# The queries' operand of a differential attention layer, made together with that of keys and values

## The chip, the cores and the metric

The kernel runs on one core of one Trainium2 chip. The core has a matrix engine (PE, whose weight loads are listed apart as PEld), a vector engine (DVE), a scalar engine (ACT), a general engine (POOL) and an engine that issues the weight DMAs (SP); each follows its own list of instructions in order, and they meet through semaphores. The metric is the device time of one execution in microseconds (us). Lower is better.

## The reference, cut to what matters

A block of four attention branches is followed by a convolution layer and a differential attention layer, each with memory attention and a gated feed-forward layer behind it. The sequence has 256 tokens, the model 1024 features. The change touches the differential layer:

```python
def shared_kv(x, kv_norm, w_k, w_v, cos, sin):
    h = rms_norm_2(x, kv_norm)
    k = apply_partial_rope((h @ w_k).reshape(B, S, 8, 2, 64), cos, sin)
    v = (h @ w_v).reshape(B, S, 8, 128)
def diff_attention(h, k, v, ...):          # h = rms_norm_2(x, norm_mix[1]), the same x
    q = apply_partial_rope((h @ w_q).reshape(B, S, 8, 2, 64), cos, sin)
    # per head: two softmaxes over 64 features, p0 - lam * p1, times v; a norm; @ w_o
```

Keys, values and queries are made of the same `x`, with the same root of the mean square, and of two gains, `kv_norm` and `norm_mix[1]`.

## The kernel before, in words

**Products.** Every operand of a product is split into a high and a low part, and a product is three products of parts. Weights come through four raw slots in the order of `weight_plan`, in chunks of 512 rows by 512 columns. For each chunk SP issues the load, ACT copies the high part (`act_chunk`, L591), DVE makes the low part (`vec_chunk`, L601), two chunks ahead of PE, and PE multiplies (L669). ACT may only split a chunk when PE has left the chunk three places ahead of it. A step below is one chunk on PE.

**A norm in front of a product.** `x` is not scaled first. `Norm.pe_turn` turns `x` on PE, 128 by 128 at a time into the `small` banks (L816), four transposes a call; ACT writes the high part of `x` times the gain (L834), DVE the low part (L846). The roots are multiplied in behind the product. `H` is one place for all such operands one after another; an operand's half may be written when the one before it has been taken by PE.

**The differential layer, before.** PE multiplies keys (`w_k`, four steps), values (`w_v`, four), queries of heads 0 to 3 (`w_q` 0, two steps) and of heads 4 to 7 (`w_q` 1, two). Keys and values read the operand `kv`. Behind the values `x` is turned again, for the operand `q` with the other gain: half 0 inside the values' last step, half 1 inside the queries' first. ACT copies products out scaled by the root (L2882 for keys and queries, L3016 for values). Keys and queries are then rotated by DVE in `attended` (L2894 to L2900), turned by PE (L731) and copied to `k_t` or `q_t` by ACT (L2875). ACT's copies of the second queries out of their product, the next split and the copies to `q_t` stand in one turn of its list.

**Groups.** Attention runs in six groups of heads (`DIFF_GROUPS`): for each half of the heads, heads 0, 1 with the later 128 tokens, heads 2, 3 with the same, then four heads with the first 128. A group has stages: PE makes scores (L2957); DVE adds the mask, takes maxima and their negatives (L3151 to L3155) for both softmaxes; ACT takes exponentials (L3072); DVE's part two makes reciprocals and the difference (L3160 to L3166); PE turns the rows (L2965); ACT copies them (L1479); PE mixes the values (L2973); ACT copies out (L3081). `weave` runs the groups in rounds: in each round each engine's list has one stage of every group under way, the start of a new group, and one step of filling. On PE and DVE the filling is the last thing in a round, on ACT the first. Counting from 0, group g starts in round g; its rows are turned in round g + 2 and its values mixed in round g + 3. The filling before is the last step of `w_q` 1, then eight steps of keys and values of the memory attention, then the steps of the output projection. When three groups are done, `finish_half` norms that half of the heads (DVE, POOL L766 to L771, DVE L3188), turns it (PE L731) and writes the projection's operand; for the second half its transposes on PE stand in round 10.

**Banks.** Four `small` banks go round in the order in which PE takes them; PE waits until the use four places earlier is released.

Of the kernel before, what the change touches and what calls it, by code (L numbers as in the profile page):

```python
# [124 lines left out]
def weight_plan(w):  # L125
# [64 lines left out]
    memory_use(0)  # L190
    feed(0)
    square(w["w_k_shared_2"])
    square(w["w_v_shared_2"])
    even(w["diff_w_q_2"][0])
    memory(1)
    square(w["diff_w_o_2"][0])
    memory_use(1)
# [91 lines left out]
class Kernel:  # L289
# [84 lines left out]
    def layout(self):  # L374
        w = self.w
        self.limit = self.top - 4 * FIRST_W
        self.vector_cols = self.sb("vector_cols", [P, N_VECTOR_ROWS])
        self.to_line()
        self.whole_conv = self.sb("whole_conv", [P, KT, S], at=self.at + 4 * KT * S)
        parts = self.sb("H", [P, 2, KT, S], F32R)  # L380
        h = parts[:, 0, :, :], parts[:, 1, :, :], parts[:, :, :, :]
        names = ["first", "merged", "conv", "ln", "mem0", "ffn0", "kv", "q", "att", "mem1", "ffn1"]
        ops = {name: Operand(name, h, before) for before, name in zip([None, *names], names)}
        self.H_first, self.H_merged, self.H_conv, self.H_ln, self.H_kv, self.H_q, self.H_att = (
            ops[name] for name in ("first", "merged", "conv", "ln", "kv", "q", "att"))
        self.H_mem, self.H_ffn = ([ops[f"{name}{layer}"] for layer in range(2)] for name in ("mem", "ffn"))
        self.w_raw = [self.sb(f"w_raw{i}", [P, CK * CN]) for i in range(self.N_RAW)]
        self.w_high, self.w_low, self.w_first, self.rooms, self.used, self.st = [], [], [], [], [], {}
        for slots, name, more in ((self.w_high, "w_high", HIGH_ROOM), (self.w_low, "w_low", LOW_ROOM)):
            for i in range(self.N_SPLIT):  # L390
                self.room(LINE // 4 - more)
                if slots is self.w_high:
                    self.w_first.append(self.sb(f"w_first{i}", [P, CK * CN], at=self.at))
                slots.append(self.sb(f"{name}{i}", [P, CK * CN + more], F32R))
        self.X, self.HN = self.sb("X", [P, NT, D]), self.sb("HN", [P, NT, D])
        self.gains_at = self.at
        self.gains = [self.sb(f"gain{i}", [P, D]) for i in range(2)]
        self.common = self.sb("common", [P, COMMON_W])
        self.ident, self.ones, self.causal, self.invfreq, self.half = (
            self.common[:, at:at + n] for at, n in (COMMON[name] for name in ("ident", "ones", "causal", "invfreq", "half")))  # L400
        self.room(432)
        self.vector_rows = self.sb("vector_rows", [N_VECTOR_ROWS, P])
        at, self.vcol = 0, {}
        for name, (*_, n) in VECTORS.items():
            self.vcol[name] = self.vector_cols[:, at:at + n]
            at += n
        self.two_roots, self.neg_lam, self.c_silu = self.stat("two roots", 2 * NT), self.stat("neg lambda", 1), self.stat("c silu", KT)
        for name in ("cos", "sin", "cos angle", "sin angle"):
            self.stat(name, NT * ROT // 2)

        def bank(name):
            return self.ctx.enter_context(self.nc.psum_tensor(name, [P, 512], F32))
        self.product = Ring("product", [bank(f"product{i}") for i in range(4)])
        self.small = Ring("small", [bank(f"small{i}") for i in range(4)])
        common_end = self.at
        self.layout_condition()
        self.at = self.after_gate
        self.layout_branches()
        self.limit = (self.top - 8 * KT * S) // LINE * LINE
        self.mem_op = Operand("mem", self.pair("mem", KT, at=self.limit))  # L420
        self.at = common_end
        self.layout_second()
        self.norms = {
            ("mem", 0): Norm(self, "mem0", self.H_mem[0]), ("ffn", 0): Norm(self, "ffn0", self.H_ffn[0]), ("after", 0): Norm(self, "kv", self.H_kv),
            ("q", 1): Norm(self, "q", self.H_q, "kv"), ("mem", 1): Norm(self, "mem1", self.H_mem[1]), ("ffn", 1): Norm(self, "ffn1", self.H_ffn[1]),
            ("after", 1): Norm(self, "final"),
        }

# [345 lines left out]
class Norm:  # L774
# [65 lines left out]
    def vec_turn(self, n):  # L840
        V = self.k.vec
        for b in range(2):
            key = (self.name, n, b)
            V.wait_ge(self.x.free(n), ("turned", key), ("operand high", key))
            for hi, lo, ps, gain in self.turned(n, b):
                V.eng.scalar_tensor_tensor(lo, ps, gain, hi.bitcast(F32), ALU.mult, ALU.subtract).then_inc(  # L846
                    *V.tells("operand_low", self.x.ready(n), self.k.small.free(key)))


WIDE_PLACES, NARROW_PLACES = (9, 13), (16, 24)  # L850
# [1423 lines left out]
def act_feed(k, layer, beside=None):  # L2274
# [41 lines left out]
    for n in range(D // CN):  # L2316
        for step in range(-(-FT // CK)):
            act_chunk(k)
            if n == 1 and step == 0 and after.x:
                after.act_turn(0)  # L2320
        if n == 0 and after.x:
            after.act_squares(n)
        if not after.x:
# [7 lines left out]
def vec_feed(k, layer, beside=None):  # L2331
# [92 lines left out]
    for n in range(D // CN):  # L2424
        for step in range(-(-FT // CK)):
            vec_chunk(k)
            if n == 1 and step == 0 and after.x:
                after.vec_turn(0)
        for t in range(NT):
            if after.x:  # L2430
                vec_add(k, (("down", layer, n), t), ("products", ("down", layer, n)), after, n, t, norm.root(t), ("root", norm.name))
# [481 lines left out]
def pe_differential(k):  # L2913
    pe = k.pe
    for step in pe_square(k, "w_k", k.H_kv, k.norms["after", 0].pe_behind(0, 1, WIDE_PLACES)):
        if step == 3:
            for t in range(NT):
                pe_turn_heads(k, "k heads", 0, t)
    for step in pe_square(k, "w_v", k.H_kv, k.norms["q", 1].pe_behind(3, 0, (4, 8))):
        if step == 0:  # L2920
            for t in range(NT):
                pe_turn_heads(k, "k heads", 1, t)

    def turn_queries(n):
        for t in range(NT):
            pe_turn_heads(k, "q heads", n, t)

    def queries(n):
        yield from pe_columns(k, ("w_q", n), k.H_q, KT, {(0, 15): lambda: turn_queries(0)} if n else k.norms["q", 1].pe_behind(0, 1, (4, 8)))

    told = {"groups": 0, "halves": 0}

    def fill():
        yield from queries(1)
        yield from pe_memory_keys(k, 1, ({(0, 26): lambda: turn_queries(1)}, {}))
        project = pe_add_to_x(k, "diff out", k.H_att, k.norms["mem", 1])
        for half in range(2):
            while told["halves"] <= half:
# [4 lines left out]
            yield  # L2943
        drain(project)
    filling = fill()
    drain(queries(0))
    next(filling)
    pe.wait_ge(("k heads", 1), "diff values")

    def group(heads, t):  # L2950
        nh, nk, key = len(heads), P * (t + 1), ("diff", heads[0], t)
# [14 lines left out]
        tr.then_inc(*pe.tells("turned", ("turned", key), k.rows.free((key, 0))))  # L2966
        yield
        bank, p = k.small.take((key, "mixed")), k.turned.of(key)
        pe.wait_ge(("turned rows", key), k.small.before((key, "mixed")))
        for i, h in enumerate(heads):  # L2970
            for j in range(t + 1):
                b = i * (t + 1) + j
# [18 lines left out]
def act_differential(k):  # L2991
    A = k.act
    for step in range(4):
        act_chunk(k)
        if step == 0:
            k.norms["after", 0].act_turn(1)
            k.norms["after", 0].act_squares(1)
        if step == 3:
            for t in range(NT):
                act_turn_heads(k, "k heads", k.k_t, 0, t)  # L3000
        if step >= 2:
            for t in range(NT):
                act_to_heads(k, "k heads", step - 2, t, ("w_k", 2 * (step - 2) + t), ("products", "w_k", step))
    for step in range(4):
        act_chunk(k)
        if step == 0:
            for t in range(NT):
                act_turn_heads(k, "k heads", k.k_t, 1, t)
        if step == 3:
            k.norms["q", 1].act_turn(0)  # L3010
        if step >= 2:
            n = step - 2
            for t in range(NT):
                bank = ("w_v", 2 * n + t)
                A.wait_ge(("root", "kv"), ("products", "w_v", step))
                A.eng.activation(k.vals[:, t, n * CN:(n + 1) * CN], k.product.of(bank)[:, 0:CN], ACT.Copy, scale=k.norms["after", 0].root(t)).then_inc(  # L3016
                    *A.tells("diff_values", "diff values", k.product.free(bank)))

    def turn_queries(n):
        for t in range(NT):  # L3020
# [2 lines left out]
    def rows_out(n):  # L3023
        for t in range(NT):
            act_to_heads(k, "q heads", n, t, (("w_q", n), t), ("products", ("w_q", n)), ("k heads", "turned"))

    told = {"groups": 0, "halves": 0}

    def fill():
        act_chunk(k)  # L3030
        turn_queries(0)
        yield
        act_chunk(k)
        yield
        rows_out(1)
        act_chunk(k)
        turn_queries(1)
        yield
        act_chunk(k)
        yield  # L3040
        act_keys_out(k, 1, 0)
        for out, n in ((act_keys_out, 1), (act_values_out, 0), (act_values_out, 1)):
            act_chunk(k)
            yield
            act_chunk(k)
# [9 lines left out]
            yield  # L3055
        drain(project)
    act_chunk(k)
    k.norms["q", 1].act_turn(1)
    act_chunk(k)
    rows_out(0)  # L3060
    filling = fill()
    next(filling)
    scale = HD ** -0.5

    def group(heads, t):
# [32 lines left out]
def vec_differential(k):  # L3098
    V = k.vec
    for step in range(4):  # L3100
        vec_chunk(k)
        if step == 0:
            k.norms["after", 0].vec_turn(1)
        if step >= 2:
            for t in range(NT):
                vec_rotate(k, "k heads", step - 2, t)
    for step in range(4):
        if step == 3:
            k.norms["q", 1].vec_turn(0)
        vec_chunk(k)  # L3110
    k.norms["q", 1].vec_turn(1)

    def queries(n):
        for step in range(2):
# [10 lines left out]

    def fill():
        yield from queries(1)
        yield from vec_chunks(k, 8)
        project = vec_add_to_x(k, "diff out", k.norms["mem", 1])
        for half in range(2):  # L3130
            while told["halves"] <= half:
# [5 lines left out]
        drain(project)  # L3137
    filling = fill()
    drain(queries(0))
    next(filling)  # L3140
    scale = HD ** -0.5

    def group(heads, t):
# [201 lines left out]
```

## Time and profile before

| what | value |
|---|---|
| device time, median of 3 runs | 1110.7 us (1110.38 to 1110.97) |
| span of the profiled execution | 1111.3 us, 0.6 above the median |
| PE busy | 98% of the span |
| DVE, ACT, POOL busy | 67%, 53%, 5% |
| mean DMA rate | 176 GB/s |
| granted clock of PE, mean | 0.997 of 2.4 GHz |

Busy time of PE counts pipelined products by their modelled ends, so short waits are best looked for in the list of waits and in the chain. The differential layer's products begin 698.5 us from the span's start and its projection ends near 862 us.

### The profile page before, as it was taken

Reading aid. Unit: us, or ns where it says so; the run is one execution under the profiler, and the core shown is the slowest. Engines: PE = TensorE matmul, PEld = TensorE weight load, DVE = VectorE, ACT = ScalarE, POOL = GpSimd, SP = SyncE. Lnnn points to the kernel's source line nnn. Section 1 sums busy time; section 2 is a strip of 40 time slices with the busy share of each in tenths; the row PEclk is TensorE's granted clock in tenths of the full one; section 3 lists DMA queues with packets and bytes.
Section 4 is the critical chain, followed back from the end, with each engine's and each line's share of the span. In section 5 each row is a group of like instructions: output and inputs, shape, how many; then the busy total and the mean of one; then the engine's idle time right before and its main releaser. Section 6 shows DMA issues by size and latency. Waiting matters only on the chain.

```text
span 1111.3 us, 15418 instructions
## 1 busy us (share of the span) xinstructions
PE 1092.0 (98%) x6251; PEld 951.6 (86%) x6251; DVE 749.5 (67%) x1024; ACT 583.6 (53%) x940; POOL 54.4 (5%) x87
## 2 busy tenths in 40 slices
PE   8999999999999999999999999999999999999997
PEld 6799988788898988989988988788988989888986
DVE  5736776865679977555678855546967546788643
ACT  3458653444477775555444544456765545444442
POOL 3311000000010000001000000000011000000000
PEclk9999999999999999999999999999999999999999
DMA  9956464655654325535555555544445435555550
GB/s 343 381 161 207 135 196 162 233 184 189 223 168 126 115 77 189 175 99 149 197 184 184 196 182 196 189 153 151 152 153 189 132 115 190 190 190 189 162 179 38
DMA packets 118776, 195.09 MB, mean 176 GB/s; under 512 B 6586, under 2 KB 39762, under 8 KB 118705
## 3 DMA queue, kind: packets, MB, share of 16 engines
q1 hardware_dynamic: 116144, 187.51, 50.7%
q0 software_dynamic: 2560, 6.60, 2.0%
q8 instruction: 49, 0.80, 0.3%
q14 instruction: 23, 0.18, 0.0%
HBM read 193.04 MB, written 1.05 MB: 175 GB/s over the span
## 4 chain that ended last, share of the span: by engine, by line
PE 83%; DVE 10%; ACT 5%; issue 1%; DMA 1%; POOL 1%; SPq 0%; DVEq 0%; ACTq 0%; POOLq 0%
PE product L669 55%; PE small L706 5%; PE product L706 5%; DVE conv_out L2719 5%; PE product L708 3%; PE small L708 3%; PE product L996 3%; ACT w_high L591 1%; ACT diagonal L2612 1%; DVE w_low L601 1%; PE small L816 1%; PE small L2081 1%; PE small L731 1%; PE small L1462 1%; PE small L1451 1%
## 5 line engine op out<-in xcount | busy, mean ns | idle before, releaser
L601 DVE TENSOR_TENSOR w_low<-w_raw,w_high 128x2048 fp32r<-128x2048 f32 (+3 forms) x160 | 350.0, 2190 | 180.2 <-ACT w_high L591 178.6
L591 ACT ACTIVATE w_high<-w_raw 128x2048 fp32r<-128x2048 f32 (+3 forms) x160 | 292.1, 1832 | 175.9 <-PE product L669 144.2
L669 PE MATMUL product<-w_high,H 128*128 128x512 f32 (+2 forms) x736 | 239.7, 393 | 0.5 <-DVE w_low L601 0.5
L669 PEld LDWEIGHTS product<-w_high,H 128*128 128x128 f32 x736 | 137.9, 188 | 26.9 <-DVE w_low L601 0.9
L669 PE MATMUL product<-H,w_high 128*128 128x256 f32 x816 | 150.9, 283 | 0.1
L669 PE MATMUL product<-w_low,H 128*128 128x512 f32 (+2 forms) x368 | 142.3, 387 | 0.0
L669 PEld LDWEIGHTS product<-H,w_high 128*128 128x128 f32 x816 | 126.6, 188 | 1.1 <-DVE w_low L601 0.5
L669 PE MATMUL product<-H,w_low 128*128 128x256 f32 x408 | 114.2, 280 | 0.0
L706 PE MATMUL product<-H,w_high 128*128 128x512 f32 x256 | 89.1, 391 | 0.0
L706 PE MATMUL small<-H,w_high 128*128 128x512 f32 x256 | 89.1, 391 | 0.0
L669 PEld LDWEIGHTS product<-w_low,H 128*128 128x128 f32 x368 | 69.3, 188 | 11.9 <-issue 0.2
L669 PEld LDWEIGHTS product<-H,w_low 128*128 128x128 f32 x408 | 76.8, 188 | 0.6 <-issue 0.2
L708 PE MATMUL product<-H,w_low 128*128 128x256 f32 x256 | 71.4, 279 | 0.0
L708 PE MATMUL small<-H,w_low 128*128 128x256 f32 x256 | 71.4, 279 | 0.0
L669 PE MATMUL product<-w_high,hidden_low 128*128 128x512 f32 x176 | 68.6, 390 | 0.0
L669 PE MATMUL product<-w_low,hidden_high 128*128 128x512 f32 x176 | 68.5, 389 | 0.0
L669 PE MATMUL product<-w_high,hidden_high 128*128 128x512 f32 x176 | 68.5, 389 | 0.0
L2719 DVE SCALAR_TENSOR_TENSOR conv_out<-conv_in,taps,conv_out 128x256 f32<-128x256 f32 x150 | 63.2, 478 | 1.2
L706 PEld LDWEIGHTS small<-H,w_high 128*128 128x128 f32 x256 | 48.1, 188 | 10.6
L706 PEld LDWEIGHTS product<-H,w_high 128*128 128x128 f32 x256 | 48.1, 188 | 10.5
L2519 PE MATMUL product<-whole_conv,w_raw 128*128 128x256 f32 x256 | 56.0, 379 | 0.0
L2519 PEld LDWEIGHTS product<-whole_conv,w_raw 128*128 128x128 f32 x256 | 48.3, 190 | 6.4
(412 smaller groups left out, 1784.3 us busy)
## 6 DMA issues: line engine op xcount, KB each, us to landing
w_raw<-in_ffn_w_gate SPq DMA_DIRECT2D x20, 1024.0 KB, 5.0
w_raw<-in_ffn_w_up SPq DMA_DIRECT2D x20, 1024.0 KB, 5.0
w_raw<-in_ffn_w_down SPq DMA_DIRECT2D x20, 1024.0 KB, 5.0
w_raw<-in_w_merge SPq DMA_DIRECT2D x16, 1024.0 KB, 5.2
w_raw<-in_w_ada SPq DMA_DIRECT2D x32, 256.0 KB, 6.5
w_raw<-in_mem_w_k SPq DMA_DIRECT2D x8, 1024.0 KB, 5.0
w_raw<-in_mem_w_v SPq DMA_DIRECT2D x8, 1024.0 KB, 5.0
w_raw<-in_conv_w_pw SPq DMA_DIRECT2D x16, 512.0 KB, 4.7
```

Of the source, the lines that this page charges most:

```text
L591: k.act.eng.activation(parts_of(k, i, j)[0], raw_of(k, i), ACT.Copy).then_inc(*k.act.tells("weights_high", ("weights high", i)))
L601: k.vec.eng.tensor_tensor(low, raw, high.bitcast(F32), ALU.subtract).then_inc(*k.vec.tells("weights_low", ("weights low", i)))
L669: mm = pe.eng.matmul(bank[:, off:off + wide], a, r, start=b not in started, stop=True, skip_group_check=True)
L706: pe.eng.matmul(bank[:, :].rearrange("p (i n) -> p i n", n=S), high[:, j, column], x.parts[:, :, first + j, :], start=first + j == 0, stop ...
L708: mm = pe.eng.matmul(bank[:, 0:S], low[:, j, column], x.high[:, first + j, :], start=False, stop=True, skip_group_check=True)
L731: tr = k.pe.eng.transpose(bank[:, i * P:(i + 1) * P], src[:, c:c + P], k.ident)
L816: tr = k.pe.eng.transpose(bank[:, j * S + t * P:j * S + (t + 1) * P], k.X[:, t, c:c + P], k.ident)
L996: mm = pe.eng.matmul(bank[:, off:off + wide], a, r, start=(name, b) not in begun, stop=True, skip_group_check=True)
L1451: mm = pe.eng.matmul(scores[:, i * nk:(i + 1) * nk], q[:, h, t * P:(t + 1) * P], kk_of(h)[:, 0:nk], start=i == 0, stop=True, skip_group_ch ...
L1462: mm = pe.eng.matmul(mixed[:, i * HD:(i + 1) * HD], p[:, b * P:(b + 1) * P], v_of(h, j), start=b == 0, stop=True, skip_group_check=True)
L2519: mm = pe.eng.matmul(bank[:, half * S:(half + 1) * S], raw[:, kt, half * P:(half + 1) * P], k.whole_conv[:, kt, :], start=kt + half == 0, ...
L2719: V.eng.scalar_tensor_tensor(y[:, f, :], src, wt, y[:, f, :], ALU.mult, ALU.add).then_inc(*V.tells("taps_vec", ("conv out", f)))
```

## The change

The operand `q` leaves the place `H` and gets one of its own, on the memory of `HN` and the two `gains` rows, which nothing else uses at that time. `x` is turned once. From the same `small` bank ACT and DVE make the operand `kv`, and then, one step later, the operand `q` with the other gain (`act_turn_queries`, `vec_turn_queries`: half 0 behind step 1 of the last feed-forward product, half 1 behind step 1 of the keys). The second norm object, with its sixteen transposes, is gone. Since queries no longer wait for values, the order of steps becomes: keys (four), queries 0, values 0, queries 1, values 1 (two each), and the weights load in that order. The queries' heads are turned inside the values' steps. The filling of the rounds becomes queries 1, values 1, then the memory's eight steps, then the projection. On ACT, the copies of the second queries to `q_t` move to the turn of filling behind the one with the copies out of the product.

```diff
-    square(w["w_v_shared_2"])
-    even(w["diff_w_q_2"][0])
+    for c in range(0, D, CN):
+        add(w["diff_w_q_2"][0], [(c, CN)])
+        add(w["w_v_shared_2"], [(c, CN)])
...
+        self.H_q = Operand("q", self.pair("H_q", KT, at=queries_at))
...
-            ("q", 1): Norm(self, "q", self.H_q, "kv"), ("mem", 1): Norm(self, "mem1", self.H_mem[1]), ("ffn", 1): Norm(self, "ffn1", self.H_ffn[1]),
...
+    def act_turn_queries(self, n):
+        A = self.k.act
+        for b in range(2):
+            A.wait_ge(("operand low", (self.name, n, b)))
+            for hi, _, ps, gain in self.queries(n, b):
+                A.eng.activation(hi, ps, ACT.Copy, scale=gain).then_inc(*A.tells("operand_high", ("queries high", n, b)))
+
+    def vec_turn_queries(self, n):
+        V = self.k.vec
+        for b in range(2):
+            V.wait_ge(("turned", (self.name, n, b)), ("queries high", n, b))
+            for hi, lo, ps, gain in self.queries(n, b):
+                V.eng.scalar_tensor_tensor(lo, ps, gain, hi.bitcast(F32), ALU.mult, ALU.subtract).then_inc(
+                    *V.tells("operand_low", self.k.H_q.ready(n), self.k.small.free((self.name, n, b))))
...
@@ pe_differential
-    for step in pe_square(k, "w_v", k.H_kv, k.norms["q", 1].pe_behind(3, 0, (4, 8))):
+    def values(n):
+        yield from pe_columns(k, ("w_v", n), k.H_kv, KT, {(0, 17): lambda: turn_queries(n)})
+    for step in queries(0):
         if step == 0:
             for t in range(NT):
                 pe_turn_heads(k, "k heads", 1, t)
+    drain(values(0))
     def fill():
         yield from queries(1)
-        yield from pe_memory_keys(k, 1, ({(0, 26): lambda: turn_queries(1)}, {}))
+        yield from values(1)
+        yield from pe_memory_keys(k, 1)
@@ act_differential
     def fill():
         act_chunk(k)
-        turn_queries(0)
         yield
         act_chunk(k)
         yield
         rows_out(1)
         act_chunk(k)
+        yield
         turn_queries(1)
-        yield
         act_chunk(k)
         yield
-        act_keys_out(k, 1, 0)
-        for out, n in ((act_keys_out, 1), (act_values_out, 0), (act_values_out, 1)):
+        values_out(1)
+        for out, n in ((act_keys_out, 0), (act_keys_out, 1), (act_values_out, 0), (act_values_out, 1)):
             act_chunk(k)
             yield
             act_chunk(k)
             yield
             out(k, 1, n)
...
+    turn_queries(0)
+    act_chunk(k)
+    values_out(0)
     filling = fill()
-    next(filling)
@@ vec_differential
     def fill():
         yield from queries(1)
-        yield from vec_chunks(k, 8)
+        yield from vec_chunks(k, 10)
...
     drain(queries(0))
-    next(filling)
+    drain(vec_chunks(k, 2))
```

In the changed list of PE, the mixing of a group also waits for the values of its half, and the scores of a group wait for the copies to `q_t` of its half, as before.

## Rows read from the trace of the kernel before

**Rows 1.** The page: busy time, share of the span and instructions of each engine.

```profile
PE 1092.0 (98%) x6251; PEld 951.6 (86%) x6251; DVE 749.5 (67%) x1024; ACT 583.6 (53%) x940; POOL 54.4 (5%) x87
```

**Rows 2.** Waits of PE, 745 to 820 and 820 to 900: total, times, longest.

```profile
PE small L2957 <- DVE drows L3151: 0.8, 1, 0.8
...
PE small L731 <- DVE attended L3188: 0.2, 1, 0.2
```

**Rows 3.** The chain that ended last, 741 to 763: start, us, what, count.

```profile
741.65 0.44 PE small L816 x4
742.09 0.94 PE product L669 x4
...
749.84 12.51 PE product L669 x55
```

**Rows 4.** Timeline of ACT, 679 to 752: start, us, what, [idle before, releaser].

```profile
679.72 1.92 ACT L591 ACTIVATE w_high<-w_raw 128x2048 fp32r<-128x2048 f32 x1 [2.59 <-PE product L669]
...
750.12 1.57 ACT L834 ACTIVATE H<-small,vector_cols 128x256 fp32r<-128x256 f32 x4
```

**Rows 5.** Timeline of DVE, 681 to 753.

```profile
681.66 2.29 DVE L601 TENSOR_TENSOR w_low<-w_raw,w_high 128x2048 fp32r<-128x2048 f32 x1 [2.08 <-ACT w_high L591]
...
751.09 1.66 DVE L846 SCALAR_TENSOR_TENSOR H<-small,vector_cols,H 128x256 fp32r<-128x256 f32 x4 [2.56 <-ACT H L834]
```

**Rows 6.** Timeline of DVE, 772 to 781.

```profile
772.84 0.23 DVE L2894 TENSOR_TENSOR rotated<-attended,stats 128x64 f32<-128x64 f32 x1 [3.12 <-ACT attended L2882]
...
774.85 2.28 DVE L601 TENSOR_TENSOR w_low<-w_raw,w_high 128x2048 fp32r<-128x2048 f32 x1
777.17 0.17 DVE L3160 RECIPROCAL stats<-stats 128x2 f32<-128x2 f32 x1
...
778.60 0.69 DVE L3151 TENSOR_TENSOR drows<-small,common 128x512 f32<-128x512 f32 x1
...
780.25 0.69 DVE L3151 TENSOR_TENSOR drows<-small,common 128x512 f32<-128x512 f32 x1
```

**Rows 7.** Timeline of ACT, 767 to 792.

```profile
767.31 1.28 ACT L3072 ACT_TABLE_LOAD   x1
...
772.05 1.27 ACT L2882 ACTIVATE attended<-product,stats 128x512 f32<-128x512 f32 x2 [1.21 <-PE product L669]
...
776.79 1.09 ACT L2875 ACTIVATE q_t<-small 128x512 f32<-128x512 f32 x2 [1.67 <-PE small L731]
...
787.19 0.40 ACT L3072 ACTIVATE drows<-drows,stats 128x128 f32<-128x128 f32 x1 [1.76 <-DVE stats L3155]
...
790.52 1.23 ACT L2030 ACTIVATE mem_keys<-product 128x512 f32<-128x512 f32 x2
```

**Rows 8.** The chain that ended last, 765 to 790.

```profile
765.28 1.07 PE small L2957 x8
766.35 5.68 PE product L669 x24
...
781.00 1.71 PE small L2957 x16
...
788.50 0.89 PE small L2973 x8
789.39 0.44 PE small L2965 x4
```

**Rows 9.** Timeline of ACT, 827 to 829.

```profile
827.34 1.91 ACT L591 ACTIVATE w_high<-w_raw 128x2048 fp32r<-128x2048 f32 x1 [2.84 <-PE product L669]
```

**Rows 10.** Timeline of DVE, 839 to 841.

```profile
839.80 0.69 DVE L3188 TENSOR_TENSOR attended<-attended,stats 128x512 f32<-128x512 f32 x1 [1.52 <-POOL stats L771]
```

**Rows 11.** Windows: us, busy us (instructions) PE, PEld, DVE, ACT, POOL, clock, DMA.

```profile
189.00:192.40 3.40, 3.40 (x14) 3.03 (x13) 2.46 (x12) 0.26 (x1) 0.00 (x0) 0.50 1.02 393
1100.00:1107.00 7.00, 4.73 (x21) 3.57 (x20) 2.25 (x3) 2.07 (x5) 1.44 (x3) 1.00 0.00 0
1107.00:1111.00 4.00, 0.00 (x0) 0.00 (x0) 0.75 (x1) 0.72 (x1) 0.72 (x2) 0.53 0.64 262
```

More of the change, by code:

```diff
@@ L381, in layout @@
         h = parts[:, 0, :, :], parts[:, 1, :, :], parts[:, :, :, :]
-        names = ["first", "merged", "conv", "ln", "mem0", "ffn0", "kv", "q", "att", "mem1", "ffn1"]
+        names = ["first", "merged", "conv", "ln", "mem0", "ffn0", "kv", "att", "mem1", "ffn1"]
         ops = {name: Operand(name, h, before) for before, name in zip([None, *names], names)}
-        self.H_first, self.H_merged, self.H_conv, self.H_ln, self.H_kv, self.H_q, self.H_att = (
-            ops[name] for name in ("first", "merged", "conv", "ln", "kv", "q", "att"))
+        self.H_first, self.H_merged, self.H_conv, self.H_ln, self.H_kv, self.H_att = (
+            ops[name] for name in ("first", "merged", "conv", "ln", "kv", "att"))
         self.H_mem, self.H_ffn = ([ops[f"{name}{layer}"] for layer in range(2)] for name in ("mem", "ffn"))
@@ L394, in layout @@
                 slots.append(self.sb(f"{name}{i}", [P, CK * CN + more], F32R))
-        self.X, self.HN = self.sb("X", [P, NT, D]), self.sb("HN", [P, NT, D])
+        self.X = self.sb("X", [P, NT, D])
+        queries_at = self.at
+        self.HN = self.sb("HN", [P, NT, D])
         self.gains_at = self.at
         self.gains = [self.sb(f"gain{i}", [P, D]) for i in range(2)]
+        self.H_q = Operand("q", self.pair("H_q", KT, at=queries_at))
+        assert queries_at % LINE == 0 and queries_at + 8 * KT * S == self.at
         self.common = self.sb("common", [P, COMMON_W])
@@ L424, in layout @@
             ("mem", 0): Norm(self, "mem0", self.H_mem[0]), ("ffn", 0): Norm(self, "ffn0", self.H_ffn[0]), ("after", 0): Norm(self, "kv", self.H_kv),
-            ("q", 1): Norm(self, "q", self.H_q, "kv"), ("mem", 1): Norm(self, "mem1", self.H_mem[1]), ("ffn", 1): Norm(self, "ffn1", self.H_ffn[1]),
+            ("mem", 1): Norm(self, "mem1", self.H_mem[1]), ("ffn", 1): Norm(self, "ffn1", self.H_ffn[1]),
             ("after", 1): Norm(self, "final"),
@@ L846, in vec_turn, with queries @@
                 V.eng.scalar_tensor_tensor(lo, ps, gain, hi.bitcast(F32), ALU.mult, ALU.subtract).then_inc(
-                    *V.tells("operand_low", self.x.ready(n), self.k.small.free(key)))
+                    *V.tells("operand_low", self.x.ready(n), ("operand low", key), self.k.small.free(key)))
+    def queries(self, n, b):
+        for j in range(2):
+            f = CK * n + 2 * b + j
+            q = self.k.H_q
+            yield q.high[:, f, :], q.low[:, f, :], self.k.small.of((self.name, n, b))[:, j * S:(j + 1) * S], self.k.vcol["q"][:, f:f + 1]
+    def act_turn_queries(self, n):
[11 more added lines that the diff above has]
+                    *V.tells("operand_low", self.k.H_q.ready(n), self.k.small.free((self.name, n, b))))
 WIDE_PLACES, NARROW_PLACES = (9, 13), (16, 24)
@@ L2320, in act_feed @@
                 after.act_turn(0)
+            if n == 1 and step == 1 and after.x:
+                after.act_turn_queries(0)
         if n == 0 and after.x:
@@ L2428, in vec_feed @@
                 after.vec_turn(0)
+            if n == 1 and step == 1 and after.x:
+                after.vec_turn_queries(0)
         for t in range(NT):
@@ L2918, in pe_differential @@
                 pe_turn_heads(k, "k heads", 0, t)
-    for step in pe_square(k, "w_v", k.H_kv, k.norms["q", 1].pe_behind(3, 0, (4, 8))):
-        if step == 0:
-            for t in range(NT):
-                pe_turn_heads(k, "k heads", 1, t)
     def turn_queries(n):
@@ L2928, in queries @@
     def queries(n):
-        yield from pe_columns(k, ("w_q", n), k.H_q, KT, {(0, 15): lambda: turn_queries(0)} if n else k.norms["q", 1].pe_behind(0, 1, (4, 8)))
+        yield from pe_columns(k, ("w_q", n), k.H_q, KT)
+    def values(n):
+        yield from pe_columns(k, ("w_v", n), k.H_kv, KT, {(0, 17): lambda: turn_queries(n)})
+    for step in queries(0):
+        if step == 0:
+            for t in range(NT):
+                pe_turn_heads(k, "k heads", 1, t)
+    drain(values(0))
     told = {"groups": 0, "halves": 0}
@@ L2945, in pe_differential @@
     filling = fill()
-    drain(queries(0))
-    next(filling)
-    pe.wait_ge(("k heads", 1), "diff values")
+    pe.wait_ge(("k heads", 1))
     def group(heads, t):
@@ L2968, in group @@
         bank, p = k.small.take((key, "mixed")), k.turned.of(key)
-        pe.wait_ge(("turned rows", key), k.small.before((key, "mixed")))
+        pe.wait_ge(("turned rows", key), ("diff values", heads[0] // 4), k.small.before((key, "mixed")))
         for i, h in enumerate(heads):
@@ L2997, in act_differential @@
             k.norms["after", 0].act_squares(1)
+        if step == 1:
+            k.norms["after", 0].act_turn_queries(1)
         if step == 3:
@@ L3003, in act_differential @@
                 act_to_heads(k, "k heads", step - 2, t, ("w_k", 2 * (step - 2) + t), ("products", "w_k", step))
[L3004 to L3017, printed above, removed]
     def turn_queries(n):
@@ L3025, in rows_out, with values_out @@
             act_to_heads(k, "q heads", n, t, (("w_q", n), t), ("products", ("w_q", n)), ("k heads", "turned"))
+    def values_out(n):
+        for t in range(NT):
+            bank = (("w_v", n), t)
+            A.wait_ge(("root", "kv"), ("products", ("w_v", n)))
+            A.eng.activation(k.vals[:, t, n * CN:(n + 1) * CN], k.product.of(bank)[:, 0:CN], ACT.Copy, scale=k.norms["after", 0].root(t)).then_inc(
+                *A.tells("diff_values", ("diff values", n), k.product.free(bank)))
     told = {"groups": 0, "halves": 0}
@@ L3057, in act_differential @@
     act_chunk(k)
-    k.norms["q", 1].act_turn(1)
+    for t in range(NT):
+        act_turn_heads(k, "k heads", k.k_t, 1, t)
     act_chunk(k)
     rows_out(0)
+    act_chunk(k)
+    turn_queries(0)
+    act_chunk(k)
+    values_out(0)
     filling = fill()
-    next(filling)
     scale = HD ** -0.5
@@ L3103, in vec_differential @@
             k.norms["after", 0].vec_turn(1)
+        if step == 1:
+            k.norms["after", 0].vec_turn_queries(1)
         if step >= 2:
@@ L3106, in vec_differential @@
                 vec_rotate(k, "k heads", step - 2, t)
[L3107 to L3111, printed above, removed]
     def queries(n):
@@ L3139, in vec_differential @@
     drain(queries(0))
-    next(filling)
+    drain(vec_chunks(k, 2))
     scale = HD ** -0.5
```

## Prediction

> **What bounds the kernel now.** I read the page first: PE is busy 98% of the span [rows 1], so time is won by giving PE less to do or by taking a wait of PE away, and lost by a new wait. Next the list of PE's waits over the differential layer: from 745 to 820 one entry stands there, the scores of group 2, held 0.8 us by DVE's mask; behind 820 one of 0.2 us, the last transposes of the attended rows, held by DVE's scaling [rows 2]. Then the chain through the layer, which is nearly all PE products, and last the timelines of ACT and DVE, to see in which order each comes to the work that PE waits for. The reader should see that ACT and DVE, though half idle, work down fixed lists: PE's two waits are waits for a place in DVE's list.
>
> **The transposes that go.** Four calls of four transposes leave PE: in the chain each is 0.44 us, and four products between two of them take 0.94 us, where 55 plain ones in 12.51 make 0.91 for four [rows 3]. That is 4 x 0.44 = 1.76, with the disturbance 4 x 0.03 more; bounds 1.76 and 1.88, I take 1.9. All of it lies on PE, where nothing covers it. A transpose costs 0.11 us here. The Trainium skill (TensorE: Matmul & The Clock Gate, Part 4: PE-mode transpose) gives about 0.275 us in a kernel for a bf16 one of the same size; by that figure sixteen would save 4.4 us and the sum below would come out near 1109.4 us. The rows decide here.
>
> **The work that moves.** ACT's and DVE's conversions for the queries stay as many: a half costs ACT 1.57 us [rows 4] and DVE 1.66 [rows 5]. For half 0 they move into the last feed-forward product, behind a split, where ACT was idle 2.59 us, until PE released a slot [rows 4], and DVE 2.08 us [rows 5]. DVE has 0.4 us to spare and its split is two chunks ahead of PE, so I put this at nothing; without that cover it would be at most 1.6. Half 1 goes into the keys, where the same cadence of steps leaves more. The loads change their order, not their number or size; SP's queue stays four slots ahead. At nothing, too: the new memory place, which has no earlier user to wait for.
>
> **The first rounds.** Let T be the end of PE's last product of queries 1. Before, that is 772.03 (766.35 + 5.68 [rows 8]) and lies in round 0; after, queries 1 fill rounds 0 and 1, so T ends round 1. The wait of 0.8 came because DVE, after T, had to rotate queries 1, split a chunk, do group 0's part two and only then reach group 1's mask [rows 6], whose bank group 2's scores take. After, part two of group 0 and the masks of group 1 stand in round 1 ahead of the rotation. This wait goes: -0.8. A range for it is 0 to 0.8.
>
> **The next wait.** What is late next is the copy to `q_t` of queries 1. DVE's list behind T is the same sequence with each group one higher: rotate at T + 0.8, split at T + 2.8, part two of group 1 at T + 5.1, masks of group 2 at T + 6.6 and T + 8.2 [rows 6]. ACT's list behind T is: copy the queries out (T + 0.0 to 1.3, 772.05 [rows 7]), split, turned rows of group 0, exponentials of group 2 (round 2), and only then, in round 3, the copies to `q_t`. The exponentials of a softmax start when its maxima are ready, one mask interval (1.65) behind its mask, and the eight of group 2 lasted 790.52 - 787.19 = 3.3 in two halves of 1.65 [rows 7]. So the last of them ends at T + 8.2 + 1.65 + 1.65 = T + 11.5, and the copies to `q_t` (1.09 [rows 7]) at T + 12.6. Before, the same copies ran at 776.79, which is T + 4.8, because they stood ahead of the exponentials.
>
> PE behind T: turn group 0's rows 0.44, scores of group 2 1.71 [rows 8], step 0 of values 1 with the queries' eight transposes (24 x 0.2275 = 5.46 [rows 3], and 0.88), mix group 0 0.89, turn group 1 0.44 [rows 8]: T + 9.8. Then it comes to group 3's scores, whose heads are those of queries 1, and stands until T + 12.6: **+2.8**. Queued behind it on PE are step 1 of values 1 and everything else. Lower bound 0.5, if DVE did its split of 2.28 ahead of the rotation; upper 4.5, if one more mask interval of 1.65 came in between; I take the list as it stands. In later rounds I see no further wait there: with each PE round over 6 us (5.68 + 0.89 + 0.44 [rows 8] and scores), ACT and DVE have caught up by round 4.
>
> Does ACT reach T in time? The first scores start 13.5 before T (two times 1.07 + 5.68 [rows 8]). From that start ACT copies values 0 out (about 1.2, like the queries' 1.27) and splits (1.9), then loads its table and does group 0's exponentials: 767.31 to 770.84 (772.05 less its 1.21 idle), 3.5 [rows 7], so 6.7. DVE's part two (1.43) and masks (3.3) of group 1 follow [rows 6], and a last half of exponentials about 1.2: 12.6. So ACT is free 0.8 to 0.9 ahead of T.
>
> **The end of the groups.** In round 8 ACT's turn of filling was a split alone, 827.34, right when PE ended a step [rows 9]; after, it begins with the memory keys' copies, 1.23 for two, the next operation 1.1 behind their start [rows 7]. Behind it queue the copies of group 5's output, from which a chain runs over DVE and POOL to the scaling at 839.80 [rows 10] that PE already waited 0.2 us for in round 10 [rows 2]. PE's cover (rounds 8 and 9) stays, so the shift comes on top: **+1.1**, with bounds 0 and 1.2. Before, the keys' and values' copies stood in the odd rounds; the two more steps of values have moved them to the even ones.
>
> **The sum.** -1.9 - 0.8 + 2.8 + 1.1 = +1.2 us. On the profiled span that is 1111.3 + 1.2 = 1112.5; that execution lies 0.6 above the median, so against the runs shown 1110.7 + 1.2 = **1111.9 us**. A difference up to 0.2% (2.2 us, about what a measurement of this kernel can tell from none) is called no change: 1108.5 to 1112.9.
>
> **The rivals.**
>
> *The saving survives.* If neither wait appears, PE gains 1.9 + 0.8 = 2.7: 1108.0 us, faster. For it: both new waits come from the order of ACT's list, and if ACT gets the copies to `q_t` done within PE's 9.8 us, nothing is lost. Against it: the exponentials of group 2 need maxima that DVE cannot give sooner than T + 8.2. If the first is away and only the second stays, it is 1109.1, still no change.
>
> *The clock falls in the new wait: slower.* PE's granted clock fell to half once in the kernel, for 3.4 us from 189.0, in a stretch of small products on a busy PE; and at the end, where PE's last product ended at 1104.73, it was full up to 1107 and at 0.53 (half for nearly all of it) in the four us behind [rows 11]. So 2.3 us of idle PE were borne, and somewhat more were not; the new wait of 2.8 lies there, and behind it come products. Price: 3.4 us at half (1.2 GHz) loses 1.7 us: 1113.6, which is where it passes 1112.9; a stretch of 2.0 us at half would be enough for that. Against it: in the layer itself the clock never fell, with a wait of 0.8. The Trainium skill (TensorE: Matmul & The Clock Gate, HAM oscillation) warns that idle gaps in front of matmuls bring the clock back to half; the end of this trace agrees, no row here shows it for a gap of this length between products.
>
> *ACT misses T.* If ACT's exponentials of group 1 run past T by x, the copies out, the rotation, and the copies to `q_t` all go x later, one for one. The margin is 0.8; from 1.0 more than that the sum passes 1112.9. For it: the chain to 12.6 is long; against it, every part of it is a row. Some 1114 at worst.
>
> **How the numbers follow.** Forecast (both waits, clock kept, 1110.6 to 1112.9): 0.55. Saving survives whole, around 1108.0: 0.13; in part, 1108.6 to 1110.5: 0.10. Clock falls, 1113.6: 0.14. ACT misses T, 1113 to 1114: 0.08. Faster 0.13, the same 0.55 + 0.10 = 0.65, slower 0.22. The range runs from the first rival's 1108.0 to the clock's 1113.8 (1113.6 and a little); it leaves out half of the first rival, and a part of the last two, under 0.2.
>
> **What would show it.** PE's transposes of `x` (L816) are sixteen fewer. Among PE's waits stands one of scores (L2957) on ACT's `q_t` (L2875), near 2.8 us, with ACT's copies some 12.6 us behind the end of queries 1; the scores' wait on DVE's mask is gone; the last transposes (L731) wait some 1.1 us longer on DVE's scaling. Wrong would be: no wait on `q_t`, a granted clock below full in the layer, or PE waiting for low parts of weights.

## The result

The changed kernel takes 1113.18 us (median of 17 runs, 1110.86 to 1115.98) where the kernel before takes 1110.76 (17 runs, 1110.02 to 1114.72). The ratio is 1.0018, 95% interval 1.0011 to 1.0025: 1.2 to 2.8 us more, 2.0 in the middle. (The ratio is not the quotient of the two medians, which is 1.0022.) The forecast was 1111.9, 0.1% more, in a range of 1108.0 to 1113.8. The median lies in that range, 1.3 us above the forecast and 0.3 us above 1112.9, where "no change" was to end. The ratio stays inside 0.2%; its interval excludes 1, so the changed kernel is slower.

### The profile page after: what moved, and what is told of

Same layout as the page of the kernel before. It is cut to its first block, busy times and chain, and to the rows that moved or that the text cites. A ratio compares the mean times of both kernels' runs of the same rounds, so it can differ in the third digit from the quotient of the medians.

```text
span 1114.7 us, 15383 instructions
## 1 busy us (share of the span) xinstructions
PE 1095.4 (98%) x6235; PEld 954.0 (86%) x6235; DVE 749.4 (67%) x1024; ACT 583.7 (52%) x940; POOL 54.1 (5%) x87
## 4 chain that ended last, share of the span: by engine, by line
PE 83%; DVE 9%; ACT 5%; issue 1%; POOL 1%; DMA 0%; SPq 0%; DVEq 0%; ACTq 0%; POOLq 0%
PE product L674 55%; PE small L711 5%; PE product L711 5%; DVE conv_out L2751 5%; PE product L713 3%; PE small L713 3%; PE product L1024 3%; ACT w_high L596 1%; ACT diagonal L2644 1%; DVE w_low L606 1%; PE small L2109 1%; PE product L977 1%; PE small L821 1%; PE small L736 1%; PE small L1490 1%
## 5 line engine op out<-in xcount | busy, mean ns | idle before, releaser
L674 PE MATMUL product<-w_high,H 128*128 128x512 f32 (+2 forms) x672 | 220.9, 396 | 0.5 <-DVE w_low L606 0.5
L674 PEld LDWEIGHTS product<-w_high,H 128*128 128x128 f32 x672 | 127.0, 190 | 24.9 <-DVE w_low L606 0.9
L674 PE MATMUL product<-w_low,H 128*128 128x512 f32 (+2 forms) x336 | 130.5, 388 | 0.0
L674 PEld LDWEIGHTS product<-w_low,H 128*128 128x128 f32 x336 | 63.8, 190 | 11.0 <-issue 0.2
```

The source lines that it names most:

```text
L674: mm = pe.eng.matmul(bank[:, off:off + wide], a, r, start=b not in started, stop=True, skip_group_check=True)
```

## The profile after

The page of the changed kernel: PE has sixteen instructions fewer than in [rows 1].

```profile
span 1114.7 us, 15383 instructions
...
PE 1095.4 (98%) x6235; PEld 954.0 (86%) x6235; DVE 749.4 (67%) x1024; ACT 583.7 (52%) x940; POOL 54.1 (5%) x87
```

PE's waits in the changed kernel, 745 to 820 and 820 to 900. They answer to [rows 2]: the 0.8 us on DVE's mask is gone, scores wait 2.6 us on ACT's copies to `q_t`, and the last transposes wait 1.3 us instead of 0.2.

```profile
PE small L2992 <- ACT q_t L2907: 2.6, 1, 2.6
...
PE small L736 <- DVE attended L3218: 1.3, 1, 1.3
```

The first wait is read from timelines and the chain. By the chain queries 1 end at 755.69 + 5.69 = 761.38, the T of the prediction:

```profile
755.69 5.69 PE product L674 x24
```

PE turns their heads, which the copies to `q_t` read, 6 us later (timeline of PE):

```profile
767.36 1.03 PE L736 MATMUL small<-common,attended 128*128 128x128 f32 x8
```

DVE behind that time (these lines answer to [rows 6]):

```profile
762.19 0.23 DVE L2926 TENSOR_TENSOR rotated<-attended,stats 128x64 f32<-128x64 f32 x1 [2.93 <-ACT attended L2914]
...
764.20 2.28 DVE L606 TENSOR_TENSOR w_low<-w_raw,w_high 128x2048 fp32r<-128x2048 f32 x1
766.51 0.17 DVE L3190 RECIPROCAL stats<-stats 128x2 f32<-128x2 f32 x1
...
767.95 0.69 DVE L3181 TENSOR_TENSOR drows<-small,common 128x512 f32<-128x512 f32 x1
...
769.60 0.69 DVE L3181 TENSOR_TENSOR drows<-small,common 128x512 f32<-128x512 f32 x1
```

ACT's over the same time (they answer to [rows 7]):

```profile
761.40 1.27 ACT L2914 ACTIVATE attended<-product,stats 128x512 f32<-128x512 f32 x2 [1.02 <-PE product L674]
762.55 1.91 ACT L596 ACTIVATE w_high<-w_raw 128x2048 fp32r<-128x2048 f32 x1
764.50 0.60 ACT L1507 ACTIVATE dturned<-small 128x512 f32<-128x512 f32 x1
769.60 0.40 ACT L3105 ACTIVATE drows<-drows,stats 128x128 f32<-128x128 f32 x1 [4.50 <-DVE stats L3185]
...
772.80 1.06 ACT L2907 ACTIVATE q_t<-small 128x512 f32<-128x512 f32 x2
773.75 1.90 ACT L596 ACTIVATE w_high<-w_raw 128x2048 fp32r<-128x2048 f32 x1
```

DVE's intervals are those of before (2.0, 2.3, 1.4, 1.65), each with a group one higher. ACT stands idle 4.50 us in front of the exponentials of group 2, whose maxima DVE cannot give yet, and the copies to `q_t` stand behind them: they end at 773.86. They could have been made from about 768.0, for the last 1.6 us of that idle time: in run 1 below they begin 6.6 us behind the end of queries 1, as soon as PE's transposes release them. ACT had 1.02 us to spare at the end of queries 1 (0.8 to 0.9 forecast). The chain goes on from the copies to the scores at 773.91, and the step of values 1 behind them takes 7.30 us where such a step took 5.68 [rows 8]:

```profile
772.90 0.97 ACT q_t L2907 x2
773.87 0.04 issue
773.91 1.14 PE small L2992 x8
775.05 7.30 PE product L674 x24
```

The reason for the long step is the clock, in windows of the changed kernel (columns as in [rows 11]): the wait, a stretch behind it, the next one, and a stretch far ahead of the layer.

```profile
770.73:773.91 3.18, 0.60 (x6) 0.36 (x5) 3.05 (x5) 3.18 (x15) 0.00 (x0) 1.00 0.03 11
775.39:778.80 3.41, 3.41 (x10) 2.67 (x9) 3.24 (x7) 2.80 (x9) 0.00 (x0) 0.50 0.75 290
778.80:782.20 3.40, 3.40 (x17) 2.77 (x16) 3.16 (x6) 0.75 (x4) 0.00 (x0) 1.00 0.13 11
188.30:195.10 6.80, 6.80 (x21) 5.67 (x22) 3.43 (x14) 0.26 (x1) 0.00 (x0) 0.50 0.57 215
```

The clock fell to half (1.2 GHz) for 3.4 us, 1.5 us after PE had its work again: ten products there against seventeen in the next window of equal length. The last row has nothing to do with the change: the fall that the kernel before shows from 189.0 to 192.4 [rows 11] lasted 6.8 us in this execution.

The second wait is read in round 8 of ACT. The memory keys' copies stand ahead of the split, which begins at 814.43, 1.12 behind their start; before, it was first in its round [rows 9].

```profile
813.31 1.23 ACT L2058 ACTIVATE mem_keys<-product 128x512 f32<-128x512 f32 x2 [3.87 <-PE product L674]
814.43 1.91 ACT L596 ACTIVATE w_high<-w_raw 128x2048 fp32r<-128x2048 f32 x1
816.24 1.13 ACT L3114 ACTIVATE attended<-small,stats 128x128 f32<-128x128 f32 x4
```

At its end stands DVE's scaling, which answers to [rows 10]. From the round's first operation to it were 839.80 - 827.34 = 12.5 us before; here they are 826.89 - 813.31 = 13.6.

```profile
826.89 0.69 DVE L3218 TENSOR_TENSOR attended<-attended,stats 128x512 f32<-128x512 f32 x1 [1.52 <-POOL stats L776]
```

The moved conversions cost nothing, as said: DVE's split behind that of half 0 still waits for ACT, with 0.51 us to spare.

```profile
680.36 1.65 DVE L874 SCALAR_TENSOR_TENSOR H_q_low<-small,vector_cols,H_q_high 128x256 fp32r<-128x256 f32 x4
682.51 2.29 DVE L606 TENSOR_TENSOR w_low<-w_raw,w_high 128x2048 fp32r<-128x2048 f32 x1 [0.51 <-ACT w_high L596]
```

## The experiments

**Theory:** sixteen transposes and one wait leave PE (-1.9 and -0.8), two waits made by the order of ACT's list take their place (+2.8, +1.1), and the first of them, as idle time, brings PE's clock down. **Rivals:** the time goes elsewhere (the order of weights, the memory place, transposes that were covered anyway); the second wait follows from the first; the clock falls for another reason than the wait.

**1. The copies to `q_t` ahead of group 2's exponentials.** The changed kernel with:

```diff
 act_differential
         yield
-        turn_queries(1)
         act_chunk(k)
...
     def group(heads, t):
         nh, nk, key = len(heads), P * (t + 1), ("diff", heads[0], t)
+        if (heads[0], t) == (0, 0):
+            turn_queries(1)
```

Expected: 

> The copies of the second queries to q_t stand ahead of group 2's exponentials in ACT's list. If the order of ACT's list makes the wait of 2.6 us, that wait is gone (under 0.3 us left), the clock stays full in the layer, and the time is 1110.7 - 1.9 - 0.8 + 1.1 = 1109.1 us, a ratio of 0.9985 to the kernel before. If the time was lost elsewhere (the order of the weights, the new memory place, a saving of transposes that isn't there), the time does not fall below 1110.7 us.

Measured: 1109.24 us (12 runs; before 1110.91 in 26), ratio 0.9984 (0.9974 to 0.9993). In its timeline of ACT the copies are made in time that was idle, and the exponentials still wait for DVE:

```profile
765.69 1.09 ACT L2907 ACTIVATE q_t<-small 128x512 f32<-128x512 f32 x2 [2.93 <-PE small L736]
767.25 0.40 ACT L3106 ACTIVATE drows<-drows,stats 128x128 f32<-128x128 f32 x1 [0.47 <-DVE stats L3186]
```

Its list of PE's waits from 745 to 820 is empty, the clock is full in the whole layer, and the 1.3 us at the end stay. So the first wait comes from the order of ACT's list, and the weights' order and the memory place cost nothing that can be seen.

**2. The memory's copies in the odd rounds as well.** As 1, and:

```diff
 act_differential
-        for out, n in ((act_keys_out, 0), (act_keys_out, 1), (act_values_out, 0), (act_values_out, 1)):
-            act_chunk(k)
-            yield
-            act_chunk(k)
-            yield
-            out(k, 1, n)
+        act_chunk(k)
+        yield
+        act_chunk(k)
+        yield
+        for out, n in ((act_keys_out, 0), (act_keys_out, 1), (act_values_out, 0)):
+            act_chunk(k)
+            yield
+            out(k, 1, n)
+            act_chunk(k)
+            yield
...
             next(project)
+            if half == 0:
+                act_values_out(k, 1, 1)
             yield
```

Expected: 

> As the run before, and the memory attention's copies go back to the odd rounds of ACT's list. If these copies in round 8 make the second wait (1.3 us on DVE's scaling), it is back at about 0.2 us and the time falls by another 1.1 to 1108.0 us, ratio 0.9976. If that wait has another cause, it stays at 1.3 and the time at 1109.1.

Measured: 1107.95 us (6 runs), ratio 0.9964 (0.9952 to 0.9977): faster than both kernels. PE's waits from 690 to 860 are then one ahead of the groups, which every kernel here has, and one as small as before the change [rows 2]:

```profile
PE small L821 <- DVE X L915: 1.0, 1, 1.0
PE small L736 <- DVE attended L3225: 0.2, 1, 0.2
```

**3. The memory's copies alone.** The second diff without the first. Expected: 

> The changed kernel with the memory attention's copies back in the odd rounds of ACT's list, and nothing else. If the two waits are independent, the second falls from 1.3 to 0.2 us while the one on q_t stays at 2.6 with the clock falling behind it in a part of the runs: median 1113.2 - 1.1 = 1112.1 us. If the second wait is a consequence of the first, it stays at 1.3 and the median at 1113.2.

Measured: 1112.02 us (11 runs; before 1110.54 in 27), ratio 1.0016 (1.0006 to 1.0025). PE's waits, 745 to 820 and 820 to 900:

```profile
PE small L2992 <- ACT q_t L2907: 2.6, 1, 2.6
...
PE small L736 <- DVE attended L3224: 0.2, 1, 0.2
```

The clock fell behind the wait in this trace too, 0.2 us after it, at 771.0, for 3.4 us:

```profile
770.00:776.00 6.00, 5.24 (x19) 3.85 (x20) 4.94 (x15) 4.71 (x10) 0.00 (x0) 0.72 0.53 178
```

The waits are independent: each goes with its own edit. The ratios of this run and of the changed kernel overlap; what 1.1 us is worth is shown better by runs 1 and 2, 1109.24 against 1107.95.

**4 and 5. Work for PE in the wait.** The changed kernel, in which PE does 2.6 to 2.7 us of work again in front of group 3's scores, first products, then transposes:

```diff
 pe_differential (4)
+        for again in range(4 if (heads[0], t, nh) == (0, 1, 2) else 1):
             for i, h in enumerate(heads):      # mix of values, group 0
 pe_differential (5)
-        for c in range(0, nh * nk, P):         # turned rows, group 1
+        for c in 7 * list(range(0, nh * nk, P)) if (heads[0], t) == (2, 1) else range(0, nh * nk, P):
```

Expected of 4: 

> The changed kernel, with group 0's mix of values made four times over, so that PE has 2.7 us of products ahead of the scores that it waits for (the repeats write the same numbers again). If an idle PE brings the clock down, the clock stays full there, PE's wait is under 0.4 us, and the runs lie together near 1111.9 us. If the clock falls for a reason other than idle time, it falls here too, and the median stays at 1113.2 with runs above 1115.

Expected of 5: 

> The changed kernel, with the four transposes of group 1's rows made seven times over, so that PE has 2.6 us of transposes ahead of the scores that it waits for. If any work of PE holds the clock, the runs lie near 1112.0 us as with products there; if transposes hold it less well than products, the clock falls behind them in a part of the runs and the median goes to 1113.2.

Measured: 1111.98 us (12 runs), ratio 1.0006 (0.9997 to 1.0015) with products; 1111.73 us (11 runs), 1.0013 (1.0004 to 1.0022) with transposes. The scores' wait is gone from both lists, and the clock is full, by one window of each, products first:

```profile
770.00:776.00 6.00, 6.00 (x40) 4.96 (x39) 5.65 (x13) 5.69 (x14) 0.00 (x0) 1.00 0.53 178
```

```profile
770.00:776.00 6.00, 6.00 (x34) 4.73 (x32) 5.69 (x15) 5.39 (x13) 0.00 (x0) 1.00 0.51 178
```

PE does more and gets no later: in the changed kernel it stood waiting for ACT in that time. The medians are 1.2 and 1.5 us under the changed kernel's (1.1 and 1.2 above their own runs of the kernel before, 1110.91 and 1110.54, where the changed kernel is 2.4 above its own). That agrees with a fall of the clock that is missing here, worth an estimated 1.7 us at 3.4 us of half clock. The runs do not lie as close together as expected, though (1111.07 to 1114.43 and 1110.58 to 1114.65), and both ratios overlap the changed kernel's.

**6. A longer wait.** The changed kernel with one split more ahead of the copies:

```diff
 act_differential
-        turn_queries(1)
         act_chunk(k)
+        turn_queries(1)
         yield
```

Expected: 

> The changed kernel, with one split of 1.9 us put ahead of the copies to q_t in ACT's list. If ACT's list decides, PE's wait grows from 2.6 to about 4.5 us, the clock falls behind it in nearly every run, and the median is 1111.9 + 1.9 + 1.7 = 1115.5 us. If the wait has another releaser, it stays at 2.6 us and the median at 1113.2.

Measured: 1115.24 us (8 runs, 1114.26 to 1115.99), ratio 1.0033 (1.0023 to 1.0044). PE's wait and the clock:

```profile
PE small L2992 <- ACT q_t L2907: 4.4, 1, 4.4
```

```profile
770.00:776.00 6.00, 3.23 (x11) 2.22 (x12) 3.09 (x10) 3.83 (x6) 0.00 (x0) 0.57 0.55 175
776.00:782.00 6.00, 6.00 (x26) 4.88 (x25) 5.61 (x11) 2.31 (x9) 0.00 (x0) 0.87 0.11 12
```

The wait grew by 1.8 us with a split of 1.9, and the clock fell inside it, at 770.8, and stayed at half for 6.8 us; the wait ended at 772.8. All three traces with a wait of 2.6 us or more (the changed kernel's, run 3's and this one's) show the fall in the layer; the six without such a wait (before, runs 1, 2, 4, 5 and 7) do not. One trace each is not a rate, but the two groups do not mix.

A rate can be had from the mean granted clock over the span, which was kept for every run to three places. Half clock for 3.4 us takes 0.0015 from it (half of 3.4 in 1114); the idle end of the kernel, at half for 1.3 to 4.1 us in the nine traces, takes 0.001 to 0.002 from every run. With the wait, 20 of 36 runs have a mean of 0.997 or less (9 of 17 of the changed kernel, 4 of 11 of run 3, 7 of 8 here); without it, 23 of 105 (12 of 53 of the kernel before beside the experiments, 4 of 12, 0 of 6, 1 of 12, 1 of 11 and 5 of 11 of runs 1, 2, 4, 5 and 7). So a low clock is more frequent with the wait, and rarer again where PE has work in its place. It is not confined to the wait, and a mean does not say where in the kernel the clock fell. The trace of run 3 has a fall at a mean of 0.998, so these counts miss some.

**7. The transposes twice.** The kernel before, with each transpose of `x` for the queries issued twice:

```diff
 Norm.pe_turn
             for t in range(NT):
-                tr = k.pe.eng.transpose(bank[...], k.X[:, t, c:c + P], k.ident)
+                for again in range(2 if self.name == "q" else 1):
+                    tr = k.pe.eng.transpose(bank[...], k.X[:, t, c:c + P], k.ident)
```

Expected: 

> The kernel before, with each of the sixteen transposes of x for the queries made twice in the same place. If they lie on PE without cover at 0.11 us each, the time grows by 16 x 0.11 = 1.8 us to 1112.5, ratio 1.0016. If they are covered by other work, it stays at 1110.7; by the Trainium skill's 0.275 us each (TensorE: Matmul & The Clock Gate, Part 4: PE-mode transpose) it would be 1115.1.

Measured: 1113.17 us (11 runs; before 1110.54), ratio 1.0020 (1.0011 to 1.0029), so 1.2 to 3.2 us. In its chain a call that was 0.44 us [rows 3] is:

```profile
739.17 0.87 PE small L817 x8
740.04 0.93 PE product L669 x4
740.98 0.87 PE small L817 x8
```

Four times 0.43 more is 1.7 us on PE, inside the interval; nothing covers them, and 4.4 us are outside it. Five of the eleven runs have a mean clock of 0.997 or less, against 4 of 27 of the kernel before; the other six have a median of 1112.26, 1.75 us above that of the other 23 (1110.51).

## Why the prediction was right, and where it was off

**The transposes that go** (-1.9): confirmed by count and by run 7, at 0.11 us each. In the kernel before, each transpose of `x` is nevertheless 0.27 us long (durations in ns, shortest, median and longest):

```profile
L816 PE MATMUL small<-common,X x16: 270/272/273, 741.5 to 749.6; 128*128 128x128 f32 x16
```

The 0.275 us of the Trainium skill (TensorE: Matmul & The Clock Gate, Part 4: PE-mode transpose) agrees with that length, though it is stated for bf16. It was not the price: four in a row take 0.44 us, since each begins 0.11 us after the one before it. The prediction's 4.4 us took a length for a price.

**The work that moves** (0): confirmed, with 0.51 us to spare where 0.4 was forecast.

**The first rounds** (-0.8): the wait on DVE's mask is gone.

**The next wait** (+2.8): 2.6 in the list of waits. The copies to `q_t` end 773.86 - 761.38 = 12.5 us behind the end of queries 1, where 12.6 was worked out, and run 1 shows that ACT's order makes it.

**The end of the groups** (+1.1): 1.3 - 0.2 = 1.1, undone by run 2 and by run 3.

**The sum** (+1.2) gives +1.0 with the waits as measured and the 1.9 of the rows: 2.6 + 1.1 - 0.8 - 1.9, which is 1111.8. Five of the seventeen runs lie near it, at 1110.86 to 1111.88, four of them 0.4 to 0.9 us below; the median lies at 1113.18.

**The chances** are the step that was off: the sum went by a clock that is kept. The rival in which the clock falls had 0.14 and a price of 1.7 us; in the trace it happened, and in each of the two other traces with the wait. A granted clock below full in the layer is also one of the prediction's own signs of being wrong. The range held the median because it was drawn out to this rival's price; the forecast's own band ended at 1112.9. So the path of the two waits was foreseen, and that the number lies in the range is owed to a rival that was thought unlikely.

That the median lies 1.3 us above the forecast goes with the clock. The five runs up to 1111.88 have a mean of 0.999, which leaves no room for a fall of 3.4 us; the twelve from 1112.72 have 0.995 to 0.998. That these twelve all fell in the layer is not shown: of the 53 runs of the kernel before beside the experiments, 12 have 0.997 or less as well, and these are all its runs above 1111.5. I had weighed the rival by the absence of falls in the layer before, with a wait of 0.8 us (another of 1.0 us stood ahead of the groups); the row that resembled it, the idle end of the kernel, pointed the other way. The Trainium skill (TensorE: Matmul & The Clock Gate, HAM oscillation) warns of idle gaps of PE, and the length that it names is above the 2.6 us that were enough here. The traces agree that idle time brings the clock down, but not on the length: a wait of 2.6 us brought a fall, waits of 0.8, 1.0 and 1.3 did not.

**What stays open:** the fall near 189, ahead of the layer, was 3.4 us long in the trace of before, 6.8 in that of after, and absent in all seven experiments' traces. The difference of the two profiled spans, 1114.7 - 1111.3 = 3.4, is for that part not the change's. In every run whose span was kept, the time of the run is 1.2 to 1.4 us above it. By that, the profiled execution of before took an estimated 1112.6 us, 1.9 above its median and not 0.6 as the prediction says, which is about what its fall near 189 costs (an estimated 1.7). The forecast does not hang on it, as it was made from the median. Why the clock falls near 189 was not looked into.

## What to carry to other kernels

When an operand is ready earlier, ask where its consumer's last helper stands in that helper's list: here ACT sat idle 4.5 us in front of work that could not start, with the copies that PE needed right behind it, ready for the last 1.6 us. Moving a whole stage by one round also moves everything that shared its rounds (the memory's copies), and each such item needs its own look at who is behind it. A new wait of a few microseconds on PE is to be priced with the clock that may fall behind it, not by its own length alone.

## What the runs showed of the hardware

The clock does not fall only inside the idle time: after a wait that ended at 773.91 it fell at 775.39, with PE on products, and stayed at half for 3.4 us; in run 3 it fell 0.2 us after the wait; in the longer wait of run 6 it fell while PE still stood, for 6.8 us. PE's 2.7 us of repeated products, or 2.6 us of transposes, in the same place kept it full in the traces, and made a kernel with more work on PE no slower. A transpose of 128 by 128 in f32 was 0.27 us long and cost PE 0.11 us where four stood in a row.
